# The first-weight loads of the dense expert chunks issued three chunks ahead on SyncE

## The reference, cut to what matters

```python
def one(xb):                                   # a block of tokens
    s = einsum('thcd,hcnd->thcn', (xb @ w_q), sub_keys)
    eidx, g = the 16 best of the 128 x 128 product keys of each of 8 heads, softmax of their scores
    act = gelu(einsum('td,thkd->thk', xb, u_tab[eidx]))
    coef = g * act
    return einsum('thk,thkd->td', coef, v_tab[eidx])
```

## Time and profile before

| | us |
|---|---|
| median of 3 runs | 3832.16 |
| lowest and highest of them | 3819.06, 3836.79 |
| the profiled execution's own time | 3820.58 |
| its span, first to last instruction | 3818.8 |
| TensorE busy | 3186.9 (83% of the span) |
| VectorE busy | 2681.0 (70%) |
| GpSimd busy | 1683.9 (44%) |
| ScalarE busy | 404.1 (11%) |
| bytes moved by DMA | 1021.21 MB, 267 GB/s over the span |

### The profile page before, as it was taken

The page is one execution under the profiler, slowest core; times in us unless marked ns, Lnnn a source line. Parts: engine busy times, 40 slices in busy tenths (PEclk is TensorE's granted clock), DMA queues, the critical chain, the costliest instruction groups (busy, mean ns, idle before and its releaser), DMA issues.

```text
span 3818.8 us, 57228 instructions
## 1 busy us (share of the span) xinstructions
PE 3186.9 (83%) x17422; PEld 2041.2 (53%) x17422; DVE 2681.0 (70%) x5879; ACT 404.1 (11%) x955; POOL 1683.9 (44%) x1447
## 2 busy tenths in 40 slices
PE   7948885897289999999989899893599998999997
PEld 3532122385256656656655686692356665566554
DVE  3887765367977788887766512389877788877777
ACT  1111112011111100000000100111111100000000
POOL 1446661011046655566566200010266556666674
PEclk9969997998599999999999999995699999999999
DMA  4678883412069999999999626321299999999998
GB/s 142 227 244 323 290 300 128 105 56 78 29 263 368 365 361 364 366 366 359 353 372 406 255 85 48 115 90 62 95 380 368 365 365 362 364 378 366 393 410 330
DMA packets 299184, 1021.21 MB, mean 267 GB/s; under 512 B 57805, under 2 KB 58229, under 8 KB 295870
## 3 DMA queue, kind: packets, MB, share of 16 engines
q0 software_dynamic: 188928, 687.95, 48.8%
q1 hardware_dynamic: 84928, 324.07, 22.1%
q10 hardware_dynamic: 25214, 7.72, 2.3%
HBM read 1013.90 MB, written 5.72 MB: 267 GB/s over the span
## 4 chain that ended last, share of the span: by engine, by line
PE 52%; DMA 24%; DVE 16%; issue 4%; SPq 2%; ACT 1%; DVEq 0%; POOL 0%; ACTq 0%
DMA area<-peer_ut_in 21%; PE ps L912 15%; PE ps L921 13%; PE ps L653 5%; PE ps L816 5%; PE ps L665 4%; PE ps L738 4%; DMA area<-cache_k_in,area 3%; PE ps L855 2%; DVE area L1337 2%; DVE area L1345 2%; PE ps L828 2%; DVE area L1644 1%; SPq L526 1%; DVE hn L1753 1%
## 5 line engine op out<-in xcount | busy, mean ns | idle before, releaser
L912 PE MATMUL ps<-hT,area 128*128 128x256 f32 x4096 | 968.4, 391 | 181.4 <-DMA area<-peer_ut_in 180.8
L912 PEld LDWEIGHTS ps<-hT,area 128*128 128x128 f32 x4096 | 784.6, 195 | 458.8 <-issue 356.4
L571 POOL DMA_INDIRECT area<-peer_u_in,area x396 | 529.9, 1338 | 1004.2 <-DVE area L1749 540.9
L921 PE MATMUL ps<-area 128*128 128x512 f32 x2048 | 937.2, 600 | 0.0
L571 POOL DMA_INDIRECT area<-peer_v_in,area x396 | 503.6, 1272 | 423.8 <-DVEq L1755 251.3
L921 PEld LDWEIGHTS ps<-area 128*128 128x128 f32 x2048 | 374.0, 190 | 372.7 <-issue 369.4
L1749 DVE CUSTOM_DVE_ANT_0 area<-area,hn 128x1024 f32<-128x1024 f32 x384 | 450.5, 1223 | 4.7
L1737 DVE TENSOR_TENSOR area<-area 128x256 f32<-128x256 f32 x256 | 109.3, 427 | 366.8 <-ACT area L1200 324.0
L855 PE MATMUL ps<-area 128*128 128x32 bf16 x6144 | 196.3, 179 | 163.0 <-DVE area L1644 163.0
L855 PEld LDWEIGHTS ps<-area 128*128 128x128 bf16 x6144 | 189.8, 99 | 197.6 <-issue 170.5
L653 PE MATMUL ps<-area,hT 128*128 128x512 f32 (+1 forms) x560 | 249.4, 606 | 43.4 <-DVEq L1507 36.8
(11 more groups left out here) (261 smaller groups left out, 3053.4 us busy)
## 6 DMA issues: line engine op xcount, KB each, us to landing
area<-peer_ut_in SPq DMA_DIRECT2D x256, 512.0 KB, 7.6
area<-peer_v_in SPq DMA_DIRECT2D x256, 512.0 KB
area<-wq_in SPq DMA_DIRECT2D x8, 2048.0 KB, 19.3
area<-w_in_c_in SPq DMA_DIRECT2D x6, 2048.0 KB, 7.8
area<-w_in_a_in SPq DMA_DIRECT2D x5, 2048.0 KB, 10.7
area<-peer_u_in,area POOLq DMA_INDIRECT x396, 7.2
area<-peer_v_in,area POOLq DMA_INDIRECT x396, 7.1
area<-w_out_a_in SPq DMA_DIRECT2D x2, 2048.0 KB, 10.6
```

The lines of the kernel that those rows point to most:

```text
L571: pool.indirect_dma_start(ring[r], None, ins[what + str(l)], bass.IndirectOffsetOnAxis(ap=idx[:, i:i + 1], axis=0)).then_inc(rows_landed[r ...
L912: m = pe.matmul(ps[c % 2][:, 0:DT * P], us[c][:, k, :], hT[:, k, 0:DT * P], start=(k == 0), stop=(k == KD - 1))
L921: m = pe.matmul(ps[2 + 2 * t + h][:, :], cT[:, c % 2, t * P:(t + 1) * P], vs[c % 2][:, h * 512:(h + 1) * 512], start=False, stop=False, sk ...
```

## The change

The loop on SyncE is written anew so that the u load runs three chunks ahead of the v load. At the start of a layer the u loads of chunks 0, 1 and 2 are issued; then for every n come v of chunk n and, right behind it, u of chunk n + 3. The conditions of the waits are the same as before for each load (u of chunk n needs first(n - 4) done, v of chunk n needs second(n - 2) done), and so are the slots, the sizes and the number of loads. The hardware loop has one turn less (31 instead of 32), and its last turn is written out without the three u loads that have no chunk any more. No other engine's program is touched.

```diff
-            with sp.Fori(0, NCH // CB) as j:
+            table_u, table_v = ins[f"peer_ut{l}"], ins[f"peer_v{l}"]
+
+            def u_chunk(n, row):
+                wait_apart(sp, go, first_done, n[0] + (l * NCH + n[1] + 1))
+                sp.dma_start(us[n[1] % CB], table_u[row, :, :]).then_inc(u_landed[n[1] % CB], 16)
+
+            def v_chunk(n, row):
+                wait_apart(sp, go, second_done, n[0] + (l * NCH + n[1] + 1))
+                sp.dma_start(vs[n[1] % 2], table_v[row, :]).then_inc(v_landed[n[1] % 2], 16)
+
+            for n in range(CB - 1):
+                u_chunk((0, n), slice(n * P, (n + 1) * P))
+            with sp.Fori(0, NCH // CB - 1) as j:
                 for c in range(CB):
-                    wait_apart(sp, go, first_done, j * CB + (l * NCH + c + 1))
-                    sp.dma_start(us[c], ins[f"peer_ut{l}"][bass.ds(j * (CB * P) + c * P, P), :, :])\
-                        .then_inc(u_landed[c], 16)
-                    wait_apart(sp, go, second_done, j * CB + (l * NCH + c + 1))
-                    sp.dma_start(vs[c % 2], ins[f"peer_v{l}"][bass.ds(j * (CB * P) + c * P, P), :])\
-                        .then_inc(v_landed[c % 2], 16)
+                    v_chunk((j * CB, c), bass.ds(j * (CB * P) + c * P, P))
+                    u_chunk((j * CB, c + CB - 1), bass.ds(j * (CB * P) + (c + CB - 1) * P, P))
+            for n in range(NCH - CB, NCH):
+                v_chunk((0, n), slice(n * P, (n + 1) * P))
+                if n + CB - 1 < NCH:
+                    u_chunk((0, n + CB - 1), slice((n + CB - 1) * P, (n + CB) * P))
```

## The result

The changed kernel takes 3704.6 us (median of 4 runs, 3700.5 to 3711.6) against 3825.7 us for the kernel before (4 runs): a ratio of 0.968, 95% interval 0.965 to 0.971. That is 121 us less, where 77 were forecast.

The account below looks back on a forecast made before the run. It took TensorE with waits for u to bound ranges 0 and 2, VectorE range 1, transfers range 3. Savings of 54, 4 and 19 us, together 77, took 3832.2 to 3755 us, range 3712 to 3808.

Parts of the forecast that it names:

- the mechanism: At TensorE's first: with two chunks more lead, u's 180.8 us of waits should fall to under 20.
- Range 1: Second of a layer's four 32-chunk windows: VectorE sets the pace, so only 2 us per layer, together 4, is saved.
- B: At second: the wait moves to v, which lands too late; 3780 us, chance 14%.
- C: At VectorE: gathered rows come too late because gathers share the transfer engines with the weights; 3893 us, chance 6%.
- D: Whole kernel: nothing moves, as another order between engines might hold the pace; 3832 us, chance 7%.
- A: All windows: transfers are the limit everywhere, ranges 0 and 2 staying under 370 GB/s; 3792 or 3800 us, chance 15%.
- the 8.1 us taken for ranges 0 and 2: Chunk time assumed for the first and third windows of each layer, saving together 54 us.
- the upper bound: Ranges 0 and 2 at 374 GB/s: 8.41 us per chunk, a total saving of 40 us, 3792 us.
- Range 3: Last window of each layer: transfers full, only the irregular part goes; 7.70 us per chunk, saving together 19 us.
- the case of 7.85 us: Ranges 0 and 2 at 7.85 us per chunk: total saving 109 us, 3723 us.
- its own bound for 7.65: Ranges 0 and 2 at the transfers' best rate, 7.65 us per chunk: total saving 135 us, 3697 us.

Follow-up runs that it names:

- experiment 4: The changed kernel with VectorE waiting only for the previous scaled sum of a gathered row, not each one, before starting the next: 3635.8 us, ratio 0.952.
- experiment 3: The changed kernel with the load of u(n + 3) issued in front of v(n) on SyncE instead of behind it: 3703.5 us, ratio 0.967.
- experiment 8: The changed kernel with both weight loads of a chunk cut to half: 3659.5 us in one execution.

## Why the prediction was wrong

**Right: the mechanism and the places.** The wait of L912 for u went from 180.8 us to nothing. Nothing was added on SyncE. Range 1 gave 1.6 us where I had 4, held by VectorE, as experiment 4 shows. v was not next (experiment 3), nor did the gathers starve VectorE: its waits for rows of u are 37.5 + 33.7 us in 115 pieces of at most 1.3 us, in ranges 0 and 2, which it doesn't pace, and those for rows of v 48 us, mostly in range 3. Rivals B and C are out, D by the time itself, and A by the rates: ranges 0 and 2 ran at 388 to 398 GB/s, not under 370.

**Wrong: the 8.1 us taken for ranges 0 and 2.** Ranges 0 run at 7.52 us per chunk and ranges 2 at 7.84 and 7.89. With 8.1 I had 54 us for them, and they gave 106. I took a value between the best rate that the trace showed, 409 GB/s, and the rate of range 1, 363 at share 0.97, and leaned on the second because "VectorE's one-hots and gates run beside it". Experiment 4 refutes that reason: with the one-hots there, range 1 runs at 410 GB/s once VectorE no longer holds it. Range 1 was slow in GB/s because VectorE asked for no more: six transfers of 512 KB in 8.6 us are 366 GB/s. A rate read from a stage that something else paces isn't a bound of the transfers. The same error made rival A look better than it was.

The DMA share misled in the same way. For the upper bound I scaled range 1 from share 0.97 to 1.00, as if 0.97 were nearly full, though under rival A I had noted that the same share can carry more. With packets of 173 to 175 ns it was not: by the packets of 165 ns at full pressure, range 0 of layer 0 used 352 of 410 GB/s, 86%, with a share of 0.93.

**A better sum stood in the same trace.** The waits for u in the four windows of ranges 0 and 2 of the kernel before (range 0 and 2 of layer 0, then of layer 1) are together 86 us:

```profile
PE ps L912 <- DMA area<-peer_ut_in: 22.7, 14, 2.9
PE ps L912 <- DMA area<-peer_ut_in: 22.0, 14, 2.8
PE ps L912 <- DMA area<-peer_ut_in: 20.8, 19, 2.7
PE ps L912 <- DMA area<-peer_ut_in: 20.2, 14, 2.6
```

The firsts behind a long wait that took 5.2 to 5.4 instead of 3.62 us are ten in these ranges, which is 17 us more. That is 103, and 106 came. Worked out afterwards, it fits better in sum than in its parts (28 and 21 us for range 0 of either layer and 29 and 25 for range 2, where 31, 26, 30 and 20 came), but it says that nearly all that TensorE lost where it was the pacer came back. The term that I had left out came back with it: the clock at its lower level behind a wait (granted 0.68 over the 5.37 us of the slow first in the earlier trace rows). After the change every first takes 3.62 us in the trace. The lower level isn't gone altogether: four times the gates wait 2.2 to 4.9 us for VectorE's one-hots, and the second behind them takes 5.16 to 6.08 instead of 3.67 us, at a granted clock of 0.60 to 0.71.

**Range 3** gave 8.8 us where I had 19. I took 7.70 us per chunk, and it runs at 7.84 and 7.88. It was held by transfers before, and is now, at 402 and 399 GB/s; experiment 8 shows it. The first range 3 lost its long stalls (9.0 us), the second had few to lose. In experiment 4, with VectorE faster, it reaches 7.74 and 7.76 us at 407 and 406 GB/s, so a tenth of a microsecond was VectorE's.

**Why range 0 could go below 7.65 us per chunk**, the transfers' time for 3.146 MB: it moved less. 388 GB/s x 240.7 us is 93.4 MB, and 32 chunks are 100.7. All 14 slots (four u, two v, eight rows) were full ahead of first(0). Inside the range the trace has 31 loads of u, 30 of v and 122 gathers, 183 where 32 chunks take 192, and by the bytes some five of them were still under way at its end. The rates in 40 equal parts of the range show the same, next to nothing at first and the full rate after:

```profile
GB/s 58 44 300 378 402 413 408 410 409 410 411 408 410 408 410 411 409 410 410 408 410 410 409 411 408 410 410 409 411 408 412 408 410 410 408 411 410 408 411 410
```

At 7.52 us per chunk TensorE asks for 418 GB/s, a little more than these 408 to 413, so range 0 lived in part on that store. The prediction had no such term.

**The range** ended at 3712, near the case of 7.85 us (3723), while its own bound for 7.65 was 3697. The measured 3704.6 lies between 3697 and 3712: I had worked out the lower case and left it outside the range. The median of the kernel before moved from 3832.2 to 3825.7 us with the fourth run, which is 6 of the 50 us by which the forecast missed the time.

## What to carry to other kernels

Where a wait for a transfer stands on the engine that paces a stage, and the transfers can go faster, count that wait in full, and the slow matmuls behind it too (103 us by this count, 106 measured). Where another engine or the transfers pace the stage, count little: the 49.9 us of waits for u in range 1 of both layers gave 1.6 us, the 45.3 us in range 3 gave 8.8. Take the capacity of the transfers from a stretch in which they alone set the pace, never from one in which something else does, and don't read the DMA share as a level of use: look at the packet time that share and rate give together. Here the load was late by one or two microseconds, one more chunk of lead cured it, and a second brought nothing.

## What the runs showed of the hardware

The time of a packet isn't fixed. From share and rate of one range, by the formula of experiment 4: 175 ns at 363 GB/s, 171 at 371, 168 at 383 (three ranges of the earlier trace rows), 165 at 410 (experiment 4), with the same loads and gathers in the mix. It isn't the rate alone, since range 0 of the kernel before has 173 ns at 352 GB/s. The cause of the slow ones isn't known; one-hots beside them aren't it.

A single core moved 410 GB/s for a whole range of 246.6 us (experiment 4). The limit of about 358 or 368 GB/s per core that the Trainium skill gives in "DMA: Bandwidth & Descriptors", section "Specifications", was no limit in these runs. The row with 358 gets it by halving 716 GB/s between two cores, and here one core ran.

With more lead the transfers land later and the kernel is faster: a gather takes 10.8 instead of 7.2 us to land, a load of u 8.6 instead of 7.6. What counts is whether someone waits for the landing, and VectorE's ring of eight rows had that room.
